# Gate tables in one fp32r product per token, the low part added at the eviction, five steps a body

## The chip, the cores and the metric

The kernel runs on one core of one Trainium2 chip. The metric is the device time of one execution in microseconds (us). Three executions of the kernel before took 3921.6, 3922.3 and 3922.45 us, so the median is 3922.3 us.

## The reference, cut to what matters

The model has two layers. Each is an attention block and a layer of single-row experts ("PEER"), both followed by a layer norm. The change is in the expert layer:

```python
def peer_ffn(x, wq, sub_keys, u, v):
    ...                                    # eidx: 128 chosen experts a token (8 heads x 16)
    g = jax.nn.softmax(top_s, -1)          # their gates
    def blk(inp):
        xt, et, gt = inp
        h = jnp.einsum('td,tkd->tk', xt, u[et]).astype(jnp.float32)
        a = gt * jax.nn.gelu(h, approximate=False)
        return jnp.einsum('tk,tkd->td', a.astype(v.dtype), v[et])
```

There are 128 x 128 = 16384 experts, and an expert's number is a pair of keys (i1, i2), each from 0 to 127. The sequence has 256 tokens, handled as two blocks of 128 (b = 0 and 1).

## The kernel before, in words

**No gathers.** The kernel computes every expert for every token and multiplies by a gate that is zero for the experts that a token did not choose. That needs a table of gates for each block of 128 tokens: `gates`, 128 partitions (first key) x 128 second keys x 128 tokens, with the token innermost in memory. It lies in the 16384 columns of `arena`, and one block's table is moved to DRAM before the other block's is built.

**How a table is built.** For one token, TensorE multiplies two one-hot matrices over its 128 selections: `oh1[k, i] = (first key of k is i)` and `oh2[k, i] = gate of k where the second key of k is i`. The product is that token's 128 x 128 gates. `TG = 4` tokens make one step, and `STEPS = 32` steps make a block's table. In a step GpSimd writes `oh1` (`first_keys`, four instructions on L1056), VectorE writes `oh2` (`second_keys`, four on L1514), TensorE makes four plain fp32 products of 128 columns into one PSUM bank (`gate_step`, L650), and ScalarE copies that bank into `gates` (`place_gates`, L956), where consecutive elements of one token are 512 bytes apart.

**What it runs beside.** The tables are built inside the first expert product, x times u. TensorE's fp32r format keeps fewer bits than fp32, so weights and activations are split into a high and a low part. For each half tile of u (1024 columns), ScalarE writes the high part (`split_hi`, L738), VectorE the low part (`split_lo`, L1100), and TensorE does `hidden(i, j)`: 8 products of 512 columns (L458) and 8 of 256 (L460). There are 4 buffers each for high and low, so the split of half j + 4 waits until TensorE has used half j. After each odd half ScalarE takes one part of the sum out (`take_cross`, L939), VectorE adds the other (`add_cross`, L1401), and ScalarE applies the GELU (L944).

**The order around the change.** All engines run lists written by hand, in bodies of eight halves, j = 0 to 7. The 32 bodies of a layer come in four quarters of eight. In the first and third VectorE also finds the top keys (`route_body`). The second and fourth are the build quarters, one for each block, so the program has four of them. The first body of a build quarter prepares the selections (`sel_t`, ready after j = 4) and does gate steps 0 and 1 after halves 6 and 7. Then five bodies do six steps each, at the places `STEP_OF = {0: 0, 1: 1, 3: 2, 4: 3, 6: 4, 7: 5}` (after half j, the step of that number in the body), and the last two do none. VectorE's `second_keys` for a step stands two halves ahead (`STEP_AHEAD`), and `oh1` and `oh2` have two buffers each: a step's one-hots may be written as soon as the step two before it is done.

The quantities are linked by semaphores: `oh1_done` and `oh2_done` (one-hots written), `gate_mm` (products done), `gate_evac` (bank free again). An engine that waits in its list holds everything behind the waiting instruction.

Of the kernel before, what the change touches and what calls it, by code (L numbers as in the profile page):

```python
# [15 lines left out]
P = 128  # L16
# [110 lines left out]
def build(nc, x_in, w_in, w_out, wq, keys, u_t, v_t, ln, sinks, lamp, subg, layer_consts,  # L127
# [13 lines left out]
    with ExitStack() as ctx:  # L141
# [9 lines left out]
        arena = sb("arena", [P, 16384])  # L151
        scr = sb("scr", [P, 4096])
# [85 lines left out]
        assert 2 + BUILD * PER_BODY == STEPS and BUILD < quarter - 1  # L238
        PIECES = 16
        ROWS = NKEY // PIECES  # L240
        oh1 = [scr[:, i * 512:(i + 1) * 512].rearrange("p (t n) -> p t n", n=NKEY) for i in range(2)]
        oh2 = [scr[:, 1024 + i * 512:1024 + (i + 1) * 512].rearrange("p (t n) -> p t n", n=NKEY)
               for i in range(2)]
# [5 lines left out]
        bank = [ctx.enter_context(nc.psum_tensor(f"bank{i}", [P, W], F32)) for i in range(8)]  # L249
# [33 lines left out]
        with nc.Block() as block:  # L283
            for layer in range(DEPTH):
# [18 lines left out]
                oh1_done, oh2_done, gate_mm, gate_evac = sem("oh1_done"), sem("oh2_done"), sem("gate_mm"), sem("gate_evac")  # L303
                gates_out, cols_done = sem("gates_out"), sem("cols_done")
# [120 lines left out]
                def _(pe):  # L425
# [230 lines left out]
                    for b in range(NB):  # L656
# [15 lines left out]
                        with pe.Fori(1, 1 + BUILD) as i:  # L672
                            for j in range(BODY):
                                hidden(i + (2 * b + 1) * quarter, j)
                                if j in STEP_OF:
                                    gate_step(i * PER_BODY + (b * STEPS + 2 - PER_BODY + STEP_OF[j]), STEP_OF[j] % 2)
                        with pe.Fori(1 + BUILD, quarter) as i:
                            for j in range(BODY):
                                hidden(i + (2 * b + 1) * quarter, j)
# [46 lines left out]
                def _(act):  # L726
# [246 lines left out]
                    for b in range(NB):  # L973
# [17 lines left out]
                        with act.Fori(1, 1 + BUILD) as i:  # L991
                            for j in range(BODY):
                                half_body(i + (2 * b + 1) * quarter, j)
                                if j in STEP_OF:
                                    at = 2 - PER_BODY + STEP_OF[j]
                                    place_gates(i * PER_BODY + (b * STEPS + at), i * (PER_BODY * TG) + at * TG, STEP_OF[j] % 2, b)
                        with act.Fori(1 + BUILD, quarter - (b == 1)) as i:
                            for j in range(BODY):
                                half_body(i + (2 * b + 1) * quarter, j)
# [29 lines left out]
                def _(pool):  # L1029
# [20 lines left out]
                    def first_keys(s, p, first=False):  # L1050
                        if not first:
                            pool.wait_ge(gate_mm, s - 1)
# [31 lines left out]
                def _(dve):  # L1084
# [457 lines left out]
                    STEP_AHEAD = {1: -2, 2: -1, 4: 0, 5: 1, 6: 2, 7: 3}  # L1542

                    def build_body(i, b, steps=STEP_AHEAD):

                        for j in range(BODY):
                            build_split(i, b, j)
                            if j in steps:
                                second_keys(i * PER_BODY + (b * STEPS + STEP_AHEAD[j]), STEP_AHEAD[j] % 2)

                    def first_build_body(b):

                        gate_weights(b)
                        for j in range(BODY):
# [5 lines left out]
                            if j >= 4:  # L1560
                                second_keys(b * STEPS + j - 4, j % 2, first=(b == 0 and j < 6))
# [12 lines left out]
                    for b in range(NB):  # L1574
# [3 lines left out]
                        with dve.Fori(1, BUILD) as i:  # L1578
                            build_body(i, b)
                        build_body(BUILD, b, steps=(1, 2, 4, 5))  # L1580
                        with dve.Fori(1 + BUILD, quarter - (b == 1)) as i:
                            build_body(i, b, steps=())
# [161 lines left out]
```

## Time and profile before

| | value |
|---|---|
| median of three runs | 3922.3 us |
| the profiled execution's own time | 3923.11 us |
| its span in the trace | 3921.3 us |
| TensorE (matmul) busy | 3872.0 us, 99% |
| VectorE busy | 2631.4 us, 67% |
| ScalarE busy | 2010.4 us, 51% |
| GpSimd busy | 509.5 us, 13% |
| granted TensorE clock, mean | 0.996 of 2.4 GHz |

The busy share of TensorE is that of overlapping records: a matmul's record begins when it starts and ends when its last result is out, and the next begins meanwhile. How long one takes in a row of many is therefore read from the distance between starts, and the same holds for the small overlap of VectorE's and ScalarE's records. The build quarters of the first layer lie at 679 to 823 us and at 1066 to 1210 us of the span, those of the second at 2630 to 2773 us and 3017 to 3160 us.

### The profile page before, as it was taken

To read this page: it belongs to the slowest core of one execution; us is meant where nothing else is said; L and a number is where in the kernel's file an instruction comes from. 1 tells how busy PE (TensorE), PEld (TensorE's weight loads), DVE (VectorE), ACT (ScalarE), POOL (GpSimd) and SP (SyncE) were. 2 spreads that over 40 slices of the span, in tenths; PEclk is the share of its full clock that TensorE was granted. 3 is DMA by queue.
4 is the path that set the end of the run, shared out by engine and by line. 5 is a ranking of instruction groups with operands and counts; after the bars stand their busy time and mean duration, and the time that the engine had idled before them with its cause. 6 is when DMAs were issued, how large, how long until landed. Compare 5 with 4: busy or idle time off the path is not lost.

```text
span 3921.3 us, 63614 instructions
## 1 busy us (share of the span) xinstructions
PE 3872.0 (99%) x20308; PEld 3291.4 (84%) x20308; DVE 2631.4 (67%) x4996; ACT 2010.4 (51%) x2936; POOL 509.5 (13%) x716
## 2 busy tenths in 40 slices
PE   8999999999999999999999999999999999999998
PEld 7778888988888888888787788889888988888886
DVE  7765688658865555555687566886688655555556
ACT  5674445654565444444456644456545654444443
POOL 1000001720172000000011000027102710000000
PEclk9999999999999999999999999999999999999999
DMA  6435466469645666666644454664685466666664
GB/s 226 160 140 202 174 210 211 169 203 282 216 169 205 231 229 230 229 229 229 224 172 151 148 207 175 207 206 173 213 275 205 170 216 228 229 229 229 229 230 170
DMA packets 244173, 806.64 MB, mean 206 GB/s; under 512 B 24928, under 2 KB 157536, under 8 KB 159328
## 3 DMA queue, kind: packets, MB, share of 16 engines
q1 hardware_dynamic: 207200, 771.65, 56.6%
q10 hardware_dynamic: 36864, 33.57, 2.5%
q8 instruction: 65, 1.06, 0.1%
q14 instruction: 44, 0.36, 0.0%
HBM read 752.69 MB, written 52.43 MB: 205 GB/s over the span
## 4 chain that ended last, share of the span: by engine, by line
PE 96%; DVE 2%; ACT 1%; POOL 1%; issue 0%; DMA 0%; ACTq 0%; SPq 0%; DVEq 0%; POOLq 0%
PE bank L458 27%; PE bank L460 14%; PE bank L688 12%; PE bank L690 12%; PE bank L689 12%; PE bank L472 5%; PE bank L474 5%; PE bank L473 5%; PE bank L650 3%; PE bank L500 1%; PE bank L513 1%; PE bank L529 0%; PE bank L627 0%; PE bank L485 0%; POOL scr L1056 0%; ACT hi L738 0%
## 5 line engine op out<-in xcount | busy, mean ns | idle before, releaser
L1100 DVE TENSOR_TENSOR lo<-raw,hi 128x1024 fp32r<-128x1024 f32 x1312 | 1613.5, 1230 | 1010.6 <-ACT hi L738 982.1
L738 ACT ACTIVATE hi<-raw 128x1024 fp32r<-128x1024 f32 x1312 | 1389.0, 1059 | 1464.8 <-PE bank L690 756.9
L458 PE MATMUL bank<-xhl,hi 128*128 128x512 f32 x4608 | 1199.6, 395 | 1.8 <-ACT scr L930 1.4
L458 PEld LDWEIGHTS bank<-xhl,hi 128*128 128x128 f32 x4608 | 813.7, 189 | 134.5 <-ACT scr L930 1.8
L688 PE MATMUL bank<-hi,xhl 128*128 128x512 f32 x2048 | 797.1, 389 | 3.0 <-DVE gelu_out L1401 2.7
L690 PE MATMUL bank<-hi,xhl 128*128 128x512 f32 x2048 | 796.7, 389 | 0.0
L689 PE MATMUL bank<-lo,xhl 128*128 128x512 f32 x2048 | 796.7, 389 | 0.0
L460 PEld LDWEIGHTS bank<-xhl,lo 128*128 128x128 f32 x4608 | 655.0, 190 | 64.0
L460 PE MATMUL bank<-xhl,lo 128*128 128x256 f32 x4608 | 671.6, 282 | 0.0
L688 PEld LDWEIGHTS bank<-hi,xhl 128*128 128x128 f32 x2048 | 384.4, 188 | 83.9 <-DVE gelu_out L1401 3.1
L690 PEld LDWEIGHTS bank<-hi,xhl 128*128 128x128 f32 x2048 | 384.4, 188 | 79.8
L689 PEld LDWEIGHTS bank<-lo,xhl 128*128 128x128 f32 x2048 | 384.4, 188 | 79.7
L1056 POOL TENSOR_SCALAR scr<-iota_k,small 128x128 f32<-128x128 f32 x512 | 410.7, 819 | 12.3
L472 PE MATMUL bank<-hi,xhl 128*128 128x512 f32 (+1 forms) x896 | 360.2, 402 | 3.8 <-DVE xhl L1118 3.7
L474 PE MATMUL bank<-hi,xhl 128*128 128x512 f32 (+1 forms) x896 | 349.8, 390 | 0.0
L473 PE MATMUL bank<-lo,xhl 128*128 128x512 f32 (+1 forms) x896 | 348.2, 389 | 0.0
L939 ACT ACTIVATE gelu_out<-bank 128x256 f32<-128x256 f32 x256 | 98.4, 384 | 304.7 <-PE bank L460 264.9
L472 PEld LDWEIGHTS bank<-hi,xhl 128*128 128x128 f32 x896 | 168.9, 188 | 39.0 <-issue 4.7
L474 PEld LDWEIGHTS bank<-hi,xhl 128*128 128x128 f32 x896 | 168.7, 188 | 35.8
L473 PEld LDWEIGHTS bank<-lo,xhl 128*128 128x128 f32 x896 | 169.3, 189 | 30.9
L1401 DVE TENSOR_TENSOR gelu_out<-bank,gelu_out 128x256 f32<-128x256 f32 x256 | 108.4, 423 | 119.2 <-ACT gelu_out L939 103.6
L956 ACT ACTIVATE arena<-bank 128x512 f32 (+1 forms) x128 | 142.0, 1109 | 47.4 <-ACT gelu_out L944 45.6
(153 smaller groups left out, 2208.4 us busy)
## 6 DMA issues: line engine op xcount, KB each, us to landing
raw<-u_t SPq DMA_DIRECT2D x256, 1024.0 KB, 5.0
raw<-v_t SPq DMA_DIRECT2D x256, 1024.0 KB, 4.8
raw<-w_in SPq DMA_DIRECT2D x80, 1024.0 KB, 4.8
raw<-w_out SPq DMA_DIRECT2D x32, 1024.0 KB, 4.8
raw<-wq SPq DMA_DIRECT2D x32, 1024.0 KB, 4.8
gelu_scratch<-gelu_out ACTq DMA_DIRECT2D x256, 128.0 KB, 3.7
scr<-gelu_scratch SPq DMA_DIRECT2D x256, 128.0 KB, 4.6
gates_scratch<-arena SPq DMA_DIRECT2D x32, 512.0 KB, 9.7
```

The costliest lines, as they stand in the source:

```text
L458: pe.matmul(acc[:], w, xhl[:, c, :, :].rearrange("p a t -> p (a t)"), start=(c == 0), stop=False)
L460: last = pe.matmul(acc[:, L:2 * L], w, xh[:, c, :], start=False, stop=(c == DC - 1))
L472: pe.matmul(banks[b][:, 0:width], st_h, mh, start=(c == first_c), stop=False)
L473: pe.matmul(banks[b][:, 0:width], st_h, ml, start=False, stop=False)
L474: last = pe.matmul(banks[b][:, 0:width], st_l, mh, start=False, stop=(c == last_c))
L688: pe.matmul(y, a_h, vh, start=start, stop=False)
L689: pe.matmul(y, a_h, vl, start=False, stop=False)
L690: last = pe.matmul(y, a_l, vh, start=False, stop=stop)
L738: act.activation(hi[j % NSPLIT][:], half, ACT.Copy).then_inc(hi_done, 1)
L956: act.activation(gates.rearrange("p i t -> p t i")[:, bass.ds(col, TG), :], bank[4 + p][:].rearrange("p (t i) -> p t i", t=TG), ACT.Copy). ...
L1056: last = pool.tensor_scalar(oh1[p][:, t, :], iota_k[:], key_cols[p][:, t:t + 1], None, ALU.is_equal)
L1100: dve.tensor_tensor(lo[j % NSPLIT][:], half, hi[j % NSPLIT][:].bitcast(F32), ALU.subtract).then_inc(lo_done, 1)
```

## The change

The gate is split into a high part (rounded to fp32r) and a low remainder, once for a block (`split_shares`). `oh2` of a token now is 256 columns, the high share beside the low one, written by one instruction on VectorE. TensorE makes one fp32r product of 256 columns a token. ScalarE places the high table as before, and VectorE then adds the low table from PSUM into `gates` (`add_low`), after which the banks are free. A step fills two banks, and steps alternate between two pairs. The 256-column `oh2` has room for four tokens in all, one step, and is given back by halves: two tokens of a step may be written when the same two of the step before are multiplied. `oh1` still has two buffers. Six bodies do five steps each.

```diff
-        STEP_OF = {0: 0, 1: 1, 3: 2, 4: 3, 6: 4, 7: 5}
+        STEP_OF = {0: 0, 1: 1, 3: 2, 5: 3, 6: 4}
+        PAIRS_AT = {0: 1, 1: 2, 3: 3, 5: 4, 6: 5}
+        LOW_AT = {1: 0, 2: 1, 4: 2, 6: 3, 7: 4}
...
                     def gate_step(s, p, first=False):
                         pe.wait_ge(oh1_done, s + 1)
-                        pe.wait_ge(oh2_done, s + 1)
                         if not first:
                             pe.wait_ge(gate_evac, s - 1)
-                        for t in range(TG):
-                            last = pe.matmul(bank[4 + p][:, t * P:(t + 1) * P], oh1[p][:, t, :], oh2[p][:, t, :],
-                                             start=True, stop=True)
-                        last.then_inc(gate_mm, 1)
+                        for half in range(2):
+                            pe.wait_ge(oh2_done, s * 2 + (half + 1))
+                            for t in range(2):
+                                last = pe.matmul(bank[4 + 2 * p + half][:, t * 2 * P:(t + 1) * 2 * P], oh1[p][:, 2 * half + t, :],
+                                                 oh2[:, 2 * half + t, :, :].rearrange("p r n -> p (r n)"), start=True, stop=True)
+                            last.then_inc(gate_mm, 1)
...
                     def place_gates(s, col, p, b):
-                        act.wait_ge(gate_mm, s + 1)
+                        act.wait_ge(gate_mm, s * 2 + 2)
...
-                                       bank[4 + p][:].rearrange("p (t i) -> p t i", t=TG), ACT.Copy).then_inc(gate_evac, 1)
+                                       pair_gates[p][:, 0], ACT.Copy).then_inc(gate_high, 1)
...
-                    def second_keys(s, p, first=False):
-                        if not first:
-                            dve.wait_ge(gate_mm, s - 1)
-                        for t in range(TG):
-                            col = s * TG + t
-                            last = dve.tensor_scalar(oh2[p][:, t, :], iota_k[:], sel_t[:, 1, bass.ds(col, 1)],
-                                                     sel_t[:, 2, bass.ds(col, 1)], ALU.is_equal, ALU.mult)
-                        last.then_inc(oh2_done, 1)
-
+                    def split_shares(b):
+                        gate = sel_t[:, 2, b * P:(b + 1) * P]
+                        own(mark(dve.tensor_copy(cand[:, 0:P].bitcast(F32R), gate)))
+                        own(mark(dve.tensor_tensor(cand[:, P:2 * P], gate, cand[:, 0:P], ALU.subtract)))
+
+                    def second_keys(b, s, first=False):
+                        for half in range(2):
+                            if not first:
+                                dve.wait_ge(gate_mm, s * 2 + (2 * b * STEPS + half - 1))
+                            for t in range(2 * half, 2 * half + 2):
+                                col = s * TG + t
+                                last = dve.scalar_tensor_tensor(
+                                    out=oh2[:, t], in0=iota_k[:].unsqueeze(1).to_broadcast([P, 2, NKEY]),
+                                    scalar=sel_t[:, 1, bass.ds(col + b * P, 1)],
+                                    in1=shares[:, :, bass.ds(col, 1)].to_broadcast([P, 2, NKEY]), op0=ALU.is_equal, op1=ALU.mult)
+                            last.then_inc(oh2_done, 1)
+
+                    def add_low(b, s, p):
+                        dve.wait_ge(gate_high, s + (b * STEPS + 1))
+                        cols = gates.rearrange("p i t -> p t i")[:, bass.ds(s * TG, TG), :]
+                        dve.tensor_tensor(cols, cols, pair_gates[p][:, 1], ALU.add).then_inc(gate_evac, 1)
...
                         for j in range(BODY):
                             build_split(i, b, j)
-                            if j in steps:
-                                second_keys(i * PER_BODY + (b * STEPS + STEP_AHEAD[j]), STEP_AHEAD[j] % 2)
+                            if j in LOW_AT:
+                                add_low(b, step + LOW_AT[j], (PER_BODY * odd + LOW_AT[j]) % 2)
+                            if j in PAIRS_AT and not (last and PAIRS_AT[j] == PER_BODY):
+                                second_keys(b, step + PAIRS_AT[j])
```

In the first body of a build quarter, VectorE splits the shares and writes step 0's one-hots at j = 4, step 1's at j = 6, and after j = 7 it does `add_low` of steps 0 and 1 and only then the one-hots of step 2.

On TensorE, the start of the loop's body before. L458 and L460 are one hidden half, L650 is one gate step.

```order
L458 MATMUL bank<-xhl,hi 128x512 x8
L460 MATMUL bank<-xhl,lo 128x256 x8
L645 ISA
L648 REGISTER_ALU
L650 MATMUL bank<-scr 128x128 x4
L634 REGISTER_ALU
L458 MATMUL bank<-xhl,hi 128x512 x8
L460 MATMUL bank<-xhl,lo 128x256 x8
L645 REGISTER_ALU
L648 REGISTER_ALU
L650 MATMUL bank<-scr 128x128 x4
```

The same place now; L466 and L468 are the hidden half, L659 the gate products, `one_hots` holds `oh1` and `oh2`, and `upper` is the four upper PSUM banks.

```order
L466 MATMUL bank<-xhl,hi 128x512 x8
L468 MATMUL bank<-xhl,lo 128x256 x8
L653 ISA
L655 REGISTER_ALU
L657 ISA
L659 MATMUL upper<-one_hots 128x256 x2
L657 REGISTER_ALU
L659 MATMUL upper<-one_hots 128x256 x2
L642 REGISTER_ALU
L466 MATMUL bank<-xhl,hi 128x512 x8
L468 MATMUL bank<-xhl,lo 128x256 x8
```

One run of four products became two runs of two, with a wait for VectorE ahead of each.

On VectorE, the end of a build quarter's first body before: L1514 is `second_keys` (of steps 0 to 3).

```order
L1100 TENSOR_TENSOR lo<-raw,hi 128x1024 x2
L1514 TENSOR_SCALAR scr<-iota_k,sel_t 128x128 x4
L1401 TENSOR_TENSOR gelu_out<-bank,gelu_out 128x256
L1100 TENSOR_TENSOR lo<-raw,hi 128x1024
L1514 TENSOR_SCALAR scr<-iota_k,sel_t 128x128 x4
L1100 TENSOR_TENSOR lo<-raw,hi 128x1024
L1514 TENSOR_SCALAR scr<-iota_k,sel_t 128x128 x4
L1401 TENSOR_TENSOR gelu_out<-bank,gelu_out 128x256
L1100 TENSOR_TENSOR lo<-raw,hi 128x1024
L1514 TENSOR_SCALAR scr<-iota_k,sel_t 128x128 x4
```

The same place now: L1111 is the low split, L1412 `add_cross`, L1522 and L1523 split the shares, L1531 is `second_keys` (of steps 0 to 2), L1540 is `add_low`.

```order
L1111 TENSOR_TENSOR lo<-raw,hi 128x1024 x2
L1522 CAST cand<-sel_t 128x128
L1523 TENSOR_TENSOR cand<-sel_t,cand 128x128
L1531 SCALAR_TENSOR_TENSOR one_hots<-iota_k,sel_t,cand 128x256 x4
L1412 TENSOR_TENSOR gelu_out<-bank,gelu_out 128x256
L1111 TENSOR_TENSOR lo<-raw,hi 128x1024 x2
L1531 SCALAR_TENSOR_TENSOR one_hots<-iota_k,sel_t,cand 128x256 x4
L1412 TENSOR_TENSOR gelu_out<-bank,gelu_out 128x256
L1111 TENSOR_TENSOR lo<-raw,hi 128x1024
L1540 TENSOR_TENSOR arena<-arena,upper 128x4x128 x2
L1531 SCALAR_TENSOR_TENSOR one_hots<-iota_k,sel_t,cand 128x256 x4
```

The one-hots of step 1 moved from j = 5 to j = 6, those of step 2 from j = 6 to behind j = 7, and two `add_low` stand ahead of them.

## Rows read from the trace of the kernel before

**Rows 1.** The page, busy time of each engine, its share of the span, instructions.

```profile
PE 3872.0 (99%) x20308; PEld 3291.4 (84%) x20308; DVE 2631.4 (67%) x4996; ACT 2010.4 (51%) x2936; POOL 509.5 (13%) x716
```

**Rows 2.** The page, the chain that ended last, by engine.

```profile
PE 96%; DVE 2%; ACT 1%; POOL 1%; issue 0%; DMA 0%; ACTq 0%; SPq 0%; DVEq 0%; POOLq 0%
```

**Rows 3.** Waits from 676 to 880 us: who for whom, us, times, longest.

```profile
DVE lo L1100 <- ACT hi L738: 50.1, 61, 2.2
...
PE bank L650 <- POOL scr L1056: 0.4, 1, 0.4
```

**Rows 4.** The chain from 760 to 800 us: start, us, what.

```profile
762.01 0.95 PE bank L460 x8
762.96 0.89 PE bank L650 x8
...
774.94 1.85 PE bank L458 x8
776.78 0.95 PE bank L460 x8
```

**Rows 5.** Timeline in a build body, after an even half: start, us, engine.

```profile
770.19 1.05 PE L650 MATMUL bank<-scr 128*128 128x128 f32 x8
...
770.39 1.06 ACT L738 ACTIVATE hi<-raw 128x1024 fp32r<-128x1024 f32 x1 [1.35 <-PE bank L460]
...
771.48 1.22 DVE L1100 TENSOR_TENSOR lo<-raw,hi 128x1024 fp32r<-128x1024 f32 x1 [1.11 <-ACT hi L738]
```

**Rows 6.** The same after an odd half, and VectorE behind a split.

```profile
780.57 0.39 ACT L939 ACTIVATE gelu_out<-bank 128x256 f32<-128x256 f32 x1 [1.43 <-PE bank L460]
780.85 1.05 ACT L738 ACTIVATE hi<-raw 128x1024 fp32r<-128x1024 f32 x1
...
785.35 1.23 DVE L1100 TENSOR_TENSOR lo<-raw,hi 128x1024 fp32r<-128x1024 f32 x1 [2.20 <-ACT hi L738]
786.49 1.23 DVE L1514 TENSOR_SCALAR scr<-iota_k,sel_t 128x128 f32<-128x128 f32 x4
```

**Rows 7.** Timeline of VectorE: a two-input instruction with a scalar, and adds in a row.

```profile
2044.78 0.47 DVE L1248 SCALAR_TENSOR_TENSOR sel_t<-scr,small,sel_t 128x256 f32<-128x256 f32 x1
2045.17 1.21 DVE L1100 TENSOR_TENSOR lo<-raw,hi 128x1024 fp32r<-128x1024 f32 x1
...
431.29 1.41 DVE L1396 TENSOR_TENSOR arena<-bank,arena 128x256 f32<-128x256 f32 x4
```

**Rows 8.** The same instruction beside GpSimd, which started at 87.19 us.

```profile
87.03 2.43 DVE L1248 SCALAR_TENSOR_TENSOR sel_t<-scr,small,sel_t 128x128 f32<-128x128 f32 x4
...
87.19 1.33 POOL L1041 TENSOR_TENSOR scr<-scr 128x512 f32<-128x512 f32 x1 [18.95 <-DVE scr L1141]
```

**Rows 9.** The one-hots before, by line: min/median/max ns.

```profile
L1514 DVE TENSOR_SCALAR scr<-iota_k,sel_t x512: 332/341/418, 675.6 to 3157.1; 128x128 f32<-128x128 f32 x171
...
L1056 POOL TENSOR_SCALAR scr<-iota_k,small x512: 597/602/1692, 676.0 to 3154.0; 128x128 f32<-128x128 f32 x171
```

**Rows 10.** Groups by line and shape: busy us, mean ns, idle before.

```profile
L1514 DVE TENSOR_SCALAR scr<-iota_k,sel_t 128x128 f32<-128x128 f32 x512 | 151.4, 357 | 0.0
L956 ACT ACTIVATE arena<-bank 128x512 f32 x120 | 133.1, 1109 | 45.6 <-ACT gelu_out L944 45.6
...
L1139 DVE TENSOR_TENSOR scr<-bank,arena 128x512 f32<-128x512 f32 x28 | 19.2, 686 | 11.1 <-PE bank L474 8.6 <-issue 2.5
...
L930 ACT ACTIVATE scr<-bank 128x512 f32<-128x512 f32 x16 | 9.1, 609 | 2.4 <-PE bank L627 2.4
```

**Rows 11.** Timeline at the first build quarter's opening, and one VectorE-to-TensorE hand-over.

```profile
679.46 1.16 PE L650 MATMUL bank<-scr 128*128 128x128 f32 x8 [0.36 <-POOL scr L1056]
...
679.64 3.43 POOL L1056 TENSOR_SCALAR scr<-iota_k,small 128x128 f32<-128x128 f32 x4
...
13.14 0.69 DVE L1118 TENSOR_TENSOR xhl<-scr,xhl 128x512 fp32r<-128x512 f32 x1 [0.27 <-ACT xhl L764]
13.89 0.29 PEld L472 LDWEIGHTS bank<-hi,xhl 128*128 128x128 f32 x1 [4.08 <-DVE xhl L1118]
```

More of the change, by code:

```diff
@@ L247, in build @@
         prod = [scr[:, 3584 + i * L:3584 + (i + 1) * L] for i in range(2)]
-        bank = [ctx.enter_context(nc.psum_tensor(f"bank{i}", [P, W], F32)) for i in range(8)]
+        upper = ctx.enter_context(nc.psum_tensor("upper", [P, 4 * W], F32))
+        bank = [ctx.enter_context(nc.psum_tensor(f"bank{i}", [P, W], F32)) for i in range(4)]
+        bank += [upper[:, i * W:(i + 1) * W] for i in range(4)]
+        pair_gates = [upper[:, p * 2 * W:(p + 1) * 2 * W].rearrange("p (t r i) -> p r t i", r=2, i=NKEY) for p in range(2)]
         eye_in, iota_in = (ctx.enter_context(nc.semaphore(n)) for n in ("eye_in", "iota_in"))
@@ L671, in _ @@
                                 gate_step(b * STEPS + j - 6, j % 2, first=(b == 0))
[L672 to L679, printed above, removed]
+                        with pe.Fori(0, BUILD // 2) as i:
+                            for odd in range(2):
+                                for j in range(BODY):
+                                    hidden(i * 2 + ((2 * b + 1) * quarter + 1 + odd), j)
+                                    if j in STEP_OF:
+                                        at = 2 + PER_BODY * odd + STEP_OF[j]
+                                        gate_step(i * (2 * PER_BODY) + (b * STEPS + at), at % 2)
+                        for j in range(BODY):
+                            hidden((2 * b + 2) * quarter - 1, j)
                     def products(b, j, slot, start=False, stop=False, qs=(0, 1)):
@@ L990, in _ @@
                                 place_gates(b * STEPS + j - 6, (j - 6) * TG, j % 2, b)
-                        with act.Fori(1, 1 + BUILD) as i:
-                            for j in range(BODY):
[L993 to L999, printed above, removed]
+                        with act.Fori(0, BUILD // 2) as i:
+                            for odd in range(2):
+                                for j in range(BODY):
+                                    half_body(i * 2 + ((2 * b + 1) * quarter + 1 + odd), j)
+                                    if j in STEP_OF:
+                                        at = 2 + PER_BODY * odd + STEP_OF[j]
+                                        place_gates(i * (2 * PER_BODY) + (b * STEPS + at), i * (2 * PER_BODY * TG) + at * TG, at % 2, b)
+                        if b == 0:
+                            for j in range(BODY):
+                                half_body(2 * quarter - 1, j)
                     def a_high(i, m):
@@ L1540, in build_split, with build_body @@
                             split_lo(AT_U, i + (2 * b + 1) * quarter + ahead // BODY, ahead % BODY)
[L1542 to L1544 removed]
+                    def build_body(i, b, step, odd, last=False):
                         for j in range(BODY):
                             build_split(i, b, j)
[L1548 to L1549 removed]
+                            if j in LOW_AT:
+                                add_low(b, step + LOW_AT[j], (PER_BODY * odd + LOW_AT[j]) % 2)
+                            if j in PAIRS_AT and not (last and PAIRS_AT[j] == PER_BODY):
+                                second_keys(b, step + PAIRS_AT[j])
                     def first_build_body(b):
@@ L1559, in first_build_body @@
                                 dve.wait_ge(sel_stored, b + 1)
-                            if j >= 4:
-                                second_keys(b * STEPS + j - 4, j % 2, first=(b == 0 and j < 6))
+                                split_shares(b)
+                                second_keys(b, 0, first=(b == 0))
+                            if j == 6:
+                                second_keys(b, 1)
+                        add_low(b, 0, 0)
+                        add_low(b, 1, 1)
+                        second_keys(b, 2)
                     def last_build_body():
@@ L1577, in _ @@
                         first_build_body(b)
[L1578 to L1582, printed above, removed]
+                        with dve.Fori(0, BUILD // 2 - 1) as i:
+                            for odd in range(2):
+                                build_body(i * 2 + (1 + odd), b, i * (2 * PER_BODY) + (2 + PER_BODY * odd), odd)
+                        build_body(BUILD - 1, b, STEPS - 2 * PER_BODY, 0)
+                        build_body(BUILD, b, STEPS - PER_BODY, 1, last=True)
+                        if b == 0:
+                            for j in range(BODY):
+                                build_split(quarter - 1, b, j)
                     last_build_body()
```

13 lines of the change are left out of this document (8 added, 5 removed).

## The prediction

> **What bounds the kernel now.** I read the page first. TensorE is busy 99% of the span, VectorE 67%, GpSimd 13% [rows 1], and the chain that ended last is 96% TensorE [rows 2]. The list of waits inside the first build quarter says the same more sharply: VectorE waits 61 times for ScalarE's high part, while TensorE waits once, 0.4 us, for the first one-hots [rows 3]. So a microsecond taken off TensorE there is a microsecond of the end, as long as its one-hots and low parts still come in time. Whether they do is the whole question, because the change takes work off TensorE and puts more on VectorE, with less lead.
>
> **TensorE's part.** In the chain, a hidden half takes 1.85 + 0.95 = 2.80 us, and a gate step takes 0.89 us from its first start to that of the next product [rows 4]. A new step is four fp32r products of 256 columns, each with its own weights. That is the same kind of instruction as the eight of L460, which take 0.95 us, 0.119 each [rows 4], so a step becomes 4 x 0.119 = 0.48 us. It saves 0.41 us. A build quarter has 32 steps, so 13.1 us, and the four quarters 52.5 us. If nothing came late, this would be the result.
>
> **VectorE's new prices.** The trace has no such one-hot instruction. One two-input instruction with a scalar from memory on 256 elements was followed by the next after 0.39 us (2044.78 to 2045.17) [rows 7]. Plain adds of 256 elements run at 0.33 us each (four in 1.41 us, the last record of 0.42 included), which is the lower bound. Beside a running GpSimd instruction, four of the two-input kind on only 128 elements took 2.43 us, 0.60 each [rows 8], which is the upper bound. The old one-hots, also written beside GpSimd, average 357 ns where the shortest is 332 [rows 9, 10]. I add that 0.03 to 0.39 and take **S = 0.42 us**, near the row of the same kind and size.
>
> `add_low` (**A**) reads PSUM and reads and writes the table at 512-byte steps. Contiguous, such an add of 512 elements takes 686 ns [rows 10], 0.61 from start to start. ScalarE's eviction into the same places takes 1109 ns against 609 for a contiguous one of this size [rows 10], so the steps cost it 0.50 us. The upper bound pays this for the read and for the write, 0.61 + 1.00 = 1.6 us. I take them as overlapping, 0.61 + 0.50 = **1.11 us**, close to ScalarE's own row. The Trainium skill ("Vector Engine (DVE) Microarchitecture Reference", measured stream behaviour on trn2) says that a stream that hops at every element slows its port, that read and write penalties only partly add, and gives 1.98 ns a column where all three hop. By that, A would be about 1.09 us and the total 0.2 us less. The trace agrees only through ScalarE's row.
>
> Per body VectorE then does 8 splits at 1.14 (785.35 to 786.49) [rows 6], 4 `add_cross` at 0.33, and 5 x (4S + A) = 13.95: together 24.4 us. TensorE's body is 8 x 2.80 + 5 x 0.48 = 24.8 us. VectorE fits on average, but barely, so what counts is when each piece is due.
>
> **What is late: one-hots due one half later.** There is room for one step of `oh2`, so step n + 1 is written after step n is multiplied. Most steps are two halves apart, but steps 0 and 1 of a body (after j = 0 and 1) and steps 3 and 4 (after j = 5 and 6) are one half apart. I follow the first pair, counting from the end of hidden half 0.
>
> - ScalarE starts the high split at 0.20 (770.19 to 770.39), VectorE's split starts 1.09 after that, at 1.29 [rows 5], and ends at 2.43. The one-hots stand behind it in VectorE's list. The first pair is written at 2.43 + 2S + 0.08 = 3.35, the second at 4.19.
> - TensorE does gate step 0 (0.48) and hidden half 1 (2.80), and wants step 1 at 3.28. From the end of a VectorE record to the weight load that waited for it took 0.06 (13.83 to 13.89) [rows 11]. A gate step that had waited had a record of 1.16 [rows 11] instead of 1.05 [rows 5], so I add 0.09 for a restart. The first two products end at 3.74, and the second two start at 4.34 and end at 4.58. In time it would have been 3.76, so TensorE loses **0.82 us** (4S - 0.86).
> - After j = 5 ScalarE first does `take_cross`, 0.28 us more (780.57 to 780.85) [rows 6]. The same walk gives **1.10 us** (4S - 0.58).
>
> The other three steps of a body are due after two halves, some 6 us after the step before, and come in time. GpSimd's four one-hots take 3.43 us [rows 11], and with two buffers they are due after three halves. The high split of half j + 4 has three halves of lead and stays in time. ScalarE does one eviction a body less. So a body loses 1.92 us of the 2.05 that its five steps save.
>
> **The opening of a quarter.** The first gate step waits for GpSimd as before (its start at 679.46 includes that) [rows 11]. The second now is due one half later, at about 682.8, and GpSimd's second one-hots end at 679.64 + 3.43 = 683.07 [rows 11]: 0.38 with the restart. Then the third: hidden half 7 ends at 679.46 + 0.57 + 2.80 = 682.83, and by the walk for an odd half VectorE is through its split at 682.83 + 1.57 + 1.14 = 685.54, and two `add_low` (2A) and four one-hots (4S) stand ahead. The last two products end at 689.91, where 686.97 would be in time: **2.94 us** (2A + 4S - 0.96). VectorE is then so far on that step 1 of the next body is not late. The share split costs VectorE 0.6 us where it is ahead of need.
>
> **The sum.** One quarter: -13.12 + 6 x 1.10 + 5 x 0.82 + 0.38 + 2.94 = **+0.90 us**, or in general 48S + 2A - 21.5. The four quarters make +3.6 us. Against the profiled execution's own 3923.11 us this is 3926.7. The median of the runs is 0.8 us lower, so I forecast **3926 us**. It is a difference of two sums of about 50 us: S moves it by 1.9 us for each 0.01, A by 0.8 for each 0.1.
>
> Outside the build quarters nothing changes: the table of block 0 is complete about one body later, still ahead of where SyncE's list stores it.
>
> **The rivals.**
>
> *The one-hots cost no more than plain adds.* With S = 0.33 and A = 0.61, a quarter gives 15.84 + 1.22 - 21.48 = -4.4, together -18 us: 3905. For it: the broadcast operands are nothing dear in the row of 0.39, and perhaps the scalar is cheaper here. Against it: that same row is already 0.06 above an add.
>
> *TensorE stays the bound and keeps its gain.* -52 us: 3870. For it: VectorE fits on average. Against it: one-hots cannot be written before the step ahead of them, and in the list they stand behind a split that starts at 1.29.
>
> *VectorE and GpSimd get in each other's way.* The old instruction read one tensor, the new one reads two, while GpSimd is writing its own one-hots most of the time. If each pays as in the row of 0.60 us [rows 8], a quarter costs 28.8 + 2.22 - 21.48 = +9.5. VectorE's body is then 10.4 + 12 + 5.6 = 28.0 us, over TensorE's 24.8 plus waits, which adds about 1.6: some +45 us, 3967. It decides from S = 0.44 on, where the result passes +0.2%. For it: GpSimd's instruction of 602 ns reaches 1692 [rows 9], so they do collide. Against it: VectorE's two-input split beside GpSimd still is 1.14 [rows 6], so there GpSimd paid. The Trainium skill ("SBUF — State Buffer", who interferes with whom) states that a VectorE instruction with two SBUF inputs contends with a GpSimd instruction that reads SBUF. By it, this rival is what the new one-hots invite; the trace shows it in rows 8 and not in rows 6.
>
> *`add_low` saturates VectorE.* With A = 1.6 a body of VectorE is 10.4 + 8.4 + 8.0 = 26.8 us, as long as TensorE's with its waits. The lateness is carried on, about 3 us a quarter beyond the formula's +1.9: +20 us, 3942.
>
> *The product is no cheaper.* If a 256-column product cost what the fp32 one did, only the losses would remain, 3978. Against it: L460.
>
> **How the numbers follow.** This measurement can hardly tell 0.2%, 7.8 us, from no change. My own case (S from 0.37 to 0.44) has 0.40 and gives 3916 to 3934. Cheap one-hots have 0.21, the kept gain 0.06, contention 0.14, saturation 0.15, the dear product 0.04. Faster by over 0.2% is cheap one-hots, the kept gain and a little of my own case: 0.29. Slower is contention, saturation and the dear product, less the mild ends of the first two: 0.30. Within 0.2%: 0.41. The range for 8 in 10 leaves out the kept gain, the dear product and the worst of the contention: 3900 to 3950.
>
> **What would show it.** In the profile after: L659 at 0.119 us a product; TensorE waiting on VectorE's L1531 twice a body, 0.8 and 1.1 us, and about 3 us once a quarter; L1531 at 0.42 from start to start and L1540 at 1.11; the splits never waited for. I am wrong if the waits on L1531 are absent or above 3 us a body, if TensorE waits for GpSimd in the loop, or if it waits for L1111's low part.

## The result: 0.4% slower, and the profile after

The changed kernel takes 3938.5 us (median of 6 runs, 3937.3 to 3939.0), the kernel before 3922.5 us (6 runs). The ratio is 1.0040, with a 95% interval of 1.0030 to 1.0051. That is 12.5 us above the forecast of 3926, inside its range of 3900 to 3950, outside the 3916 to 3934 of my own case, and on the side of "slower by over 0.2%", which had a chance of 0.30. One slow execution of e1 below (7754 us) and one of e3 (13799 us) are left out of every ratio.

The page of the kernel after, busy time of each engine, its share of the span, instructions. Beside [rows 1]:

```profile
PE 3848.6 (98%) x19796; PEld 3247.7 (83%) x19796; DVE 2860.7 (73%) x5132; ACT 2011.2 (51%) x2936; POOL 566.0 (14%) x716
```

TensorE's records cover 23 us less and VectorE's 229 us more. The chain that ended last [rows 2] no longer is TensorE's alone:

```profile
PE 88%; DVE 6%; ACT 2%; issue 2%; POOL 1%; DVEq 0%; DMA 0%; ACTq 0%; SPq 0%; POOLq 0%
```

In the list of waits (us in total, times, longest us) the first line is new; the second was 1.4 us for 4 times:

```profile
PE upper L659 <- DVE one_hots L1531: 33.8, 76, 2.2
...
PE upper L659 <- POOL one_hots L1067: 4.3, 8, 0.8
```

This list counts only the time in which no matmul record is open, and each record outlasts the start of the next product by 0.16 us and more. So the waits are better read from the distance of starts. The timeline of TensorE at the first quarter's opening (start, us, engine; [rows 11] is the same place before):

```profile
685.53 2.00 PE L466 MATMUL bank<-xhl,hi 128*128 128x512 f32 x8
687.37 1.11 PE L468 MATMUL bank<-xhl,lo 128*128 128x256 f32 x8
690.57 0.61 PE L659 MATMUL upper<-one_hots 128*128 128x256 f32 x2 [2.09 <-DVE one_hots L1531]
691.40 0.79 PE L659 MATMUL upper<-one_hots 128*128 128x256 f32 x2 [0.22 <-DVE one_hots L1531]
691.99 3.05 PE L466 MATMUL bank<-xhl,hi 128*128 128x512 f32 x8
694.88 1.11 PE L468 MATMUL bank<-xhl,lo 128*128 128x256 f32 x8
695.83 0.64 PE L659 MATMUL upper<-one_hots 128*128 128x256 f32 x4
696.31 2.00 PE L466 MATMUL bank<-xhl,hi 128*128 128x512 f32 x8
```

Three things are in it. The last two rows give the new price of a step, 696.31 - 695.83 = 0.48 us, as forecast. Step 2 was due at 687.37 + 0.95 = 688.32 and could have ended at 688.80. It started at 690.57 and ended at 691.99. And then eight products of 512 columns took 2.89 us (691.99 to 694.88) where they otherwise take 1.84. The stretches by engine say why (the number behind the counts is the granted clock):

```profile
692.00:694.00 2.00, 2.00 (x6) 1.61 (x6) 2.00 (x5) 1.07 (x1) 1.54 (x3) 0.50 0.04 13
694.00:700.00 6.00, 6.00 (x36) 5.29 (x36) 3.24 (x5) 3.04 (x4) 4.68 (x8) 0.98 0.07 8
```

TensorE was granted 1.2 GHz instead of 2.4 for 3.4 us behind the long wait, and the second of the late pairs already took 0.59 us (691.40 to 691.99) where it otherwise takes 0.35. So some 0.24 of the step's 3.19 us of delay is the clock's, and the rest the wait's. The half rate came in three of the four build quarters. VectorE at the same place (it was idle for 0.53 us before the split at 686.05, and not again until these one-hots were written):

```profile
686.05 1.23 DVE L1111 TENSOR_TENSOR lo<-raw,hi 128x1024 fp32r<-128x1024 f32 x1 [0.53 <-ACT hi L748]
687.20 2.55 DVE L1540 TENSOR_TENSOR arena<-arena,upper 128x512 f32<-128x512 f32 x2
689.65 1.69 DVE L1531 SCALAR_TENSOR_TENSOR one_hots<-iota_k,sel_t,cand 128x256 fp32r<-128x256 f32 x4
```

In the loop, both late steps of a body, TensorE and VectorE:

```profile
721.12 1.11 PE L468 MATMUL bank<-xhl,lo 128*128 128x256 f32 x8
722.30 0.50 PE L659 MATMUL upper<-one_hots 128*128 128x256 f32 x2
723.12 0.51 PE L659 MATMUL upper<-one_hots 128*128 128x256 f32 x2 [0.32 <-DVE one_hots L1531]
723.47 1.99 PE L466 MATMUL bank<-xhl,hi 128*128 128x512 f32 x8
...
737.43 1.11 PE L468 MATMUL bank<-xhl,lo 128*128 128x256 f32 x8
738.94 0.50 PE L659 MATMUL upper<-one_hots 128*128 128x256 f32 x2 [0.40 <-DVE one_hots L1531]
```
```profile
720.09 1.25 DVE L1111 TENSOR_TENSOR lo<-raw,hi 128x1024 fp32r<-128x1024 f32 x1
721.26 1.81 DVE L1531 SCALAR_TENSOR_TENSOR one_hots<-iota_k,sel_t,cand 128x256 fp32r<-128x256 f32 x4
```

Step 1 of the body was due at 721.12 + 0.95 = 722.07 and could end at 722.55. It ended at 723.47: 0.92 us late. The same reading of step 4 gives 1.25 us, and 1.49 in a quarter's first loop body.

The quarter's very first step (step 0 of the opening) is late too, and by more than before. GpSimd, and the step that waited for it:

```profile
677.25 3.84 POOL L1067 TENSOR_SCALAR one_hots<-iota_k,small 128x128 fp32r<-128x128 f32 x4
681.14 0.75 PE L659 MATMUL upper<-one_hots 128*128 128x256 f32 x4 [0.78 <-POOL one_hots L1067]
```

Its four one-hots took 3.84 us where they took 3.43 before (and 3.58 for step 1), and the step cost 1.03 us beyond its price, where it cost 0.54 before.

The groups by line and shape (busy us, mean ns, idle before), beside [rows 10]:

```profile
L1531 DVE SCALAR_TENSOR_TENSOR one_hots<-iota_k,sel_t,cand 128x256 fp32r<-128x256 f32 x512 | 225.3, 498 | 0.1
L966 ACT ACTIVATE arena<-upper 128x512 f32 x120 | 133.1, 1109 | 45.0 <-PE upper L659 27.8 <-ACT gelu_out L954 15.8
L1540 DVE TENSOR_TENSOR arena<-arena,upper 128x512 f32 x80 | 109.6, 1370 | 0.0
```

One one-hot instruction is 225.3 / 512 = 0.44 us, where I took 0.42. An `add_low` record is 1.37 us, 1.28 from start to start, where I took 1.11.

**The sum, from these rows.** I added up, over each quarter, what the hidden halves (2.79 us) and steps (0.48 us) took beyond their price, from start to start. Before, a half with a step took 3.69 us (771.00 to 774.69 on L458), so a step cost 0.90 and the saving is 0.42.

| us a quarter | forecast | measured, four quarters |
|---|---|---|
| saved by the products | 13.1 | 13.4 (32 x 0.42) |
| opening, step 0, beyond the 0.54 of before | 0 | 0.49 |
| opening, step 1 | 0.38 | 0.54 |
| opening, step 2 | 2.94 | 2.92 to 3.02 |
| step 4 of a body, six times | 1.10 | 1.49, then 1.24, the last 1.10 |
| step 1 of a body, five times | 0.82 | 0.91 |
| all waits | 14.0 | 16.0 |
| half-rate clock | 0 | 1.3, 1.55, 1.56, 0 |

Four quarters: 64.1 + 4.4 - 53.8 = +14.7 us. Read directly, from the half ahead of step 0 to the 56th half behind it, a quarter took 185.85 us before and 189.66, 189.93, 189.95 and 188.47 after, 14.6 us more in all. The spans differ by 15.2 us (3936.5 and 3921.3).

### The profile page after: what moved, and what is told of

The parts are those of the page before. It is cut to its first block, busy times and chain, and to the rows that moved or that the text cites. A ratio compares the mean times of both kernels' runs of the same rounds, so it can differ in the third digit from the quotient of the medians.

```text
span 3936.5 us, 62878 instructions
## 1 busy us (share of the span) xinstructions
PE 3848.6 (98%) x19796; PEld 3247.7 (83%) x19796; DVE 2860.7 (73%) x5132; ACT 2011.2 (51%) x2936; POOL 566.0 (14%) x716
## 4 chain that ended last, share of the span: by engine, by line
PE 88%; DVE 6%; ACT 2%; issue 2%; POOL 1%; DVEq 0%; DMA 0%; ACTq 0%; SPq 0%; POOLq 0%
PE bank L466 21%; PE bank L468 11%; PE bank L698 6%; PE bank L700 6%; PE bank L699 6%; PE upper L698 6%; PE upper L700 6%; PE upper L699 6%; PE bank L480 5%; PE bank L482 5%; PE bank L481 5%; DVE one_hots L1531 2%; ACT hi L748 2%; PE upper L466 2%; DVE lo L1111 1%
## 5 line engine op out<-in xcount | busy, mean ns | idle before, releaser
L1111 DVE TENSOR_TENSOR lo<-raw,hi 128x1024 fp32r<-128x1024 f32 x1312 | 1614.9, 1231 | 870.3 <-ACT hi L748 839.4
L466 PE MATMUL bank<-xhl,hi 128*128 128x512 f32 x4352 | 1111.0, 394 | 1.8 <-ACT scr L940 1.4
L466 PEld LDWEIGHTS bank<-xhl,hi 128*128 128x128 f32 x4352 | 777.8, 189 | 135.1 <-ACT scr L940 1.8
L468 PEld LDWEIGHTS bank<-xhl,lo 128*128 128x128 f32 x4352 | 608.4, 191 | 51.8
L468 PE MATMUL bank<-xhl,lo 128*128 128x256 f32 x4352 | 622.3, 282 | 0.0
L1067 POOL TENSOR_SCALAR one_hots<-iota_k,small 128x128 fp32r<-128x128 f32 x512 | 440.9, 878 | 12.3
L698 PE MATMUL bank<-hi,xhl 128*128 128x512 f32 x1024 | 398.7, 389 | 3.0 <-DVE gelu_out L1412 2.6
L700 PE MATMUL bank<-hi,xhl 128*128 128x512 f32 x1024 | 398.4, 389 | 0.0
L699 PE MATMUL bank<-lo,xhl 128*128 128x512 f32 x1024 | 398.3, 389 | 0.0
L698 PE MATMUL upper<-hi,xhl 128*128 128x512 f32 x1024 | 398.3, 389 | 0.0
L699 PE MATMUL upper<-lo,xhl 128*128 128x512 f32 x1024 | 398.3, 389 | 0.0
L700 PE MATMUL upper<-hi,xhl 128*128 128x512 f32 x1024 | 398.3, 389 | 0.0
L698 PEld LDWEIGHTS bank<-hi,xhl 128*128 128x128 f32 x1024 | 192.2, 188 | 43.9 <-DVE gelu_out L1412 3.1
L1531 DVE SCALAR_TENSOR_TENSOR one_hots<-iota_k,sel_t,cand 128x256 fp32r<-128x256 f32 x512 | 225.3, 498 | 0.1
L700 PEld LDWEIGHTS bank<-hi,xhl 128*128 128x128 f32 x1024 | 192.2, 188 | 40.1
L699 PEld LDWEIGHTS upper<-lo,xhl 128*128 128x128 f32 x1024 | 192.3, 188 | 39.9
L698 PEld LDWEIGHTS upper<-hi,xhl 128*128 128x128 f32 x1024 | 192.2, 188 | 40.0
```

The source lines that it names most:

```text
L466: pe.matmul(acc[:], w, xhl[:, c, :, :].rearrange("p a t -> p (a t)"), start=(c == 0), stop=False)
L468: last = pe.matmul(acc[:, L:2 * L], w, xh[:, c, :], start=False, stop=(c == DC - 1))
L698: pe.matmul(y, a_h, vh, start=start, stop=False)
L699: pe.matmul(y, a_h, vl, start=False, stop=False)
L700: last = pe.matmul(y, a_l, vh, start=False, stop=stop)
L1067: last = pool.tensor_scalar(oh1[p][:, t, :], iota_k[:], key_cols[p][:, t:t + 1], None, ALU.is_equal)
```

## The experiments

All ran beside the kernel before, whose medians there were 3922.8 to 3923.2 us. "The waits" of a quarter below are counted as "all waits" in the table; the changed kernel has 16.0 us. My theory was list order: TensorE waits because the one-hots stand behind a split or an add in VectorE's list while they are due one half later. Its rival was that VectorE is full.

**Early one-hots everywhere (e1_early_all).** `build_split` gets the one-hots as an argument and puts them ahead of its split, for steps 1 and 4 of each body and for steps 1 and 2 of the opening:

```diff
 def build_split(i, b, j, last=False, keys=None):
     if j % 2:
         add_cross(...)
+    if keys:
+        keys()
     split_lo(...)
...
-    build_split(i, b, j)
+    early = j in (0, 5)
+    build_split(i, b, j, keys=(lambda: second_keys(b, step + PAIRS_AT[j])) if early else None)
...
-    if j in PAIRS_AT and not (last and PAIRS_AT[j] == PER_BODY):
+    if j in PAIRS_AT and not early and not (last and PAIRS_AT[j] == PER_BODY):
         second_keys(b, step + PAIRS_AT[j])
...
-    build_split(0, b, j)
+    if j == 7:
+        add_low(b, 0, 0)
+    build_split(0, b, j, keys={6: lambda: second_keys(b, 1), 7: lambda: second_keys(b, 2)}.get(j))
...
-    if j == 6:
-        second_keys(b, 1)
-    add_low(b, 0, 0)
     add_low(b, 1, 1)
-    second_keys(b, 2)
```

> One-hots of steps 1 and 4 of a body ahead of VectorE's split, and in the first body those of steps 1 and 2 ahead of the splits, with the second low add last. List order (my theory: TensorE waits 16.0 us a quarter because the one-hots stand behind a split or an add): the waits on L1531 go, about 61 us, and with them the half-rate clock stretches, 4 us: 3873 us. Saturation (VectorE's body of 8 x 1.14 + 4 x 0.33 + 5 x 3.02 = 25.5 us is longer than TensorE's 24.8): TensorE waits for the low splits in place of the one-hots, 0.7 us a body in 24 bodies: 3890 us.

Measured: 3892.5 us, ratio to before 0.9921 (0.9901 to 0.9941). So 46 us came from the order of one list alone, and the kernel is faster than both. But 20 us of what list order alone would give (3873) is missing, and both theories have a share. The waits are 5.3 to 5.7 us a quarter. Some 1.5 us of that are steps 1 and 2 of the opening, which I had expected to vanish, 6 us in all. In the loop it is now the second pair of a step that is late, 0.3 to 0.45 us twice a body, 3.3 to 3.8 us a quarter and 14 us in all. And VectorE, over most of the first quarter, is (PE, PEld, DVE, ACT, POOL busy):

```profile
700.00:830.00 130.00, 128.95 (x759) 113.49 (x758) 129.62 (x189) 81.97 (x108) 92.10 (x131) 1.00 0.52 182
```

129.62 of 130 us. It is full. With S = 0.44 and A = 1.28 its body is 9.1 + 1.3 + 5 x 3.04 = 25.6 us against TensorE's 24.8. The loop bodies of e1 take 25.4 to 25.6 us (739.40, 764.95 and 790.31 are the starts of three), so the 14 us are VectorE's. In the changed kernel's own order that shortage was hidden by TensorE's waits, which made the body 27 us long.

**Only the loop (e2_early_loop), only the opening (e3_early_opening).** The two halves of that edit.

> Only the loop's one-hots (steps 1 and 4 of a body) ahead of the split; the opening of a quarter stays. List order: 12.3 us less a quarter, 3889 us; the wait of 3.2 us at the opening and the half-rate stretches behind it stay. Saturation: 3906 us or more.

> Only the first body of a quarter is reordered; the loop's waits of 0.9 and 1.25 us stay. List order: the 3.2 us wait goes, 0.9 us comes at step 1 of the next body, which was spared before, so 2.5 us less a quarter; if the clock falls because of that wait, the 1.1 to 1.6 us behind it in three quarters go too: 3924 us, and no half rate in the build quarters. If the clock falls for another reason (the wait for GpSimd just before, or the sum of the waits): 3928 us, with the half rate still there.

Measured: 3902.0 us (0.9947; 0.9931 to 0.9964) and 3927.5 us (1.0012; 1.0002 to 1.0022). The first lies between its two cases: in e2 the waits are 6.9 to 8.1 us a quarter, the step-2 wait is still 2.9 us in three quarters (2.1 in the fourth), and the half rate follows it in two. The second has the number of the case with the half rate, but not its cause: there is no half rate in any quarter of e3. Its waits are 14.5 us a quarter, because the step after the opening was 1.5 us late and not 0.9, and step 1 of the opening 0.74 and not 0.54, which together are 3 us. The 1.03 us at step 0, behind GpSimd, are still there, so it is not that wait that brings the half rate:

```profile
690.55 1.11 PE L468 MATMUL bank<-xhl,lo 128*128 128x256 f32 x8
692.89 0.74 PE L659 MATMUL upper<-one_hots 128*128 128x256 f32 x4 [1.23 <-DVE one_hots L1531]
693.47 2.00 PE L466 MATMUL bank<-xhl,hi 128*128 128x512 f32 x8
695.31 1.11 PE L468 MATMUL bank<-xhl,lo 128*128 128x256 f32 x8
```

After this wait of 1.5 us the next eight products still take 1.84 (693.47 to 695.31).

**A low add of 8 elements (e4_low_8).**

```diff
-dve.tensor_tensor(cols, cols, pair_gates[p][:, 1], ALU.add)
+dve.tensor_tensor(cols[:, 0, 0:8], cols[:, 0, 0:8], pair_gates[p][:, 1, 0, 0:8], ALU.add)
```

> The low add covers 8 elements instead of 512, so the low table is left out but for these; every instruction and wait stays in its place. List order: the opening's wait shrinks by two adds, 2.4 us, the first body's by 0.2, the waits of 0.9 and 1.25 us a body stay; with the clock back, 3924 us. Saturation: the loop's waits shrink too, towards 0.5 us a body: 3890 us.

Measured: 3925.4 us (1.0005; 0.9995 to 1.0015), as list order said. The opening's step 2 is 0.6 to 0.8 us late in three quarters (1.0 in the fourth) instead of 3.0, the half rate is gone, the 1.49 us of the first late step fall to 1.24, and the other waits of the loop stay at 0.91 and 1.24 us. So in the changed order the add costs the loop nothing: what is late there stands behind the split, not behind the add.

**GpSimd writes 8 columns of its one-hots (e5_pool_8).** From step 2 on:

```diff
-last = pool.tensor_scalar(oh1[p][:, t, :], iota_k[:], key_cols[p][:, t:t + 1], None, ALU.is_equal)
+last = pool.tensor_scalar(oh1[p][:, t, 0:8], iota_k[:, 0:8], key_cols[p][:, t:t + 1], None, ALU.is_equal)
```

> The changed kernel in its own order, but GpSimd writes only 8 of the 128 columns of each one-hot from step 2 on, so it hardly touches memory beside VectorE (the tables are then partly stale). If GpSimd makes VectorE's one-hots dear (contention), they fall from 0.43 to the 0.39 from start to start, and TensorE's loop waits from 0.92 and 1.25 to 0.75 and 1.1 us: 3930 us. If 0.43 is what the instruction costs (my theory), nothing moves: 3938 us.

Measured: 3930.1 us (1.0023; 1.0013 to 1.0032). This is the number of the contention theory, and mine, that 0.43 is what the instruction costs by itself, fell. The number alone would say too much, though. VectorE's one-hots by line, and a late four of them in the loop, which took 1.81 us before:

```profile
L1531 DVE SCALAR_TENSOR_TENSOR one_hots<-iota_k,sel_t,cand 128x256 fp32r<-128x256 f32 x512 | 215.5, 481 | 0.1
```
```profile
747.45 1.70 DVE L1531 SCALAR_TENSOR_TENSOR one_hots<-iota_k,sel_t,cand 128x256 fp32r<-128x256 f32 x4
```

Four now take 1.70 us, 0.41 from start to start instead of 0.44. The waits fall from 16.0 to 14.8 us in three quarters (13.9 in the fourth), which is 5 to 6 us. The half rate appears in one quarter instead of three, the other 3 us, but that is not shown to be GpSimd's doing: the opening's step 2 is 2.92 us late in the second and third quarter, as in the changed kernel, where the half rate followed. The ten executions also fall into two groups, 3928.6 to 3930.1 and 3933.5 to 3935.1 us, and the profile is of the lower one.

**A contiguous low add (e6_contig).** On top of e1_early_all:

```diff
-dve.tensor_tensor(cols, cols, pair_gates[p][:, 1], ALU.add)
+dve.tensor_tensor(pair_gates[p][:, 1], iota_k[:].unsqueeze(1).to_broadcast([P, TG, NKEY]), pair_gates[p][:, 1], ALU.add)
```

> Early one-hots as in e1_early_all, and the low add keeps its 512 elements but reads a contiguous SBUF operand and writes back to PSUM, so no operand is strided and the low part does not reach the table. Strides (my theory): the add falls from 1.28 to 0.65 us, VectorE's body from 25.5 to 22.4 us, under TensorE's 24.8; the waits of about 0.4 us twice a body that stay in e1_early_all go: 3877 us. If these waits are the hand-over between engines and not a full VectorE: 3892 us as e1_early_all.

Measured: 3879.9 us (0.9890; 0.9873 to 0.9906). The add is 685 ns, and the loop's waits are gone. What is left, 2.2 us a quarter, lies in the opening. The 12.6 us between this kernel and e1_early_all are what a full VectorE had cost, and the strides had filled it; the rest of the missing 20 us is the opening, which stays.

**High and low added up in PSUM (e7_psum_sum).** On top of e1_early_all, with `add_low` left out and `gate_evac` given by the eviction:

```diff
-    last = pe.matmul(bank[4 + 2 * p + half][:, t * 2 * P:(t + 1) * 2 * P], oh1[p][:, 2 * half + t, :],
-                     oh2[:, 2 * half + t, :, :].rearrange("p r n -> p (r n)"), start=True, stop=True)
+    for r in range(2):
+        last = pe.matmul(bank[4 + 2 * p + half][:, t * 2 * P:t * 2 * P + P], oh1[p][:, 2 * half + t, :],
+                         oh2[:, 2 * half + t, r, :], start=(r == 0), stop=(r == 1))
```

> Early one-hots as in e1_early_all, but high and low product of a token are two products of 128 columns added up in the same PSUM columns, so the low add is gone from VectorE and the whole table is kept. If a 128-column fp32r product costs TensorE half of a 256-column one (0.06 us), a step stays 0.48 us and VectorE has room: 3877 us. If it costs as much as one of 256 columns (0.12 us), a step takes 0.95 us: 3932 us. If it costs as a 128-column fp32 product (0.205 us), a step takes 1.6 us: 4020 us.

Measured: 3929.4 us (1.0016; 1.0006 to 1.0026), near the middle case. TensorE in the loop:

```profile
743.40 1.01 PE L660 MATMUL upper<-one_hots 128*128 128x128 f32 x8
744.25 2.07 PE L466 MATMUL bank<-xhl,hi 128*128 128x512 f32 x8
```

Eight products of 128 columns take 0.85 us, 0.106 each, almost what one of 256 columns takes (0.119). From half to half, a step adds 0.90 us, just as the old fp32 one did. The gain of the change is therefore that high and low lie side by side in one wide product, and not the format alone; and the low add is its price.

**Four tokens innermost (e8_t_inner_early, e9_t_inner).** The token is innermost in the table, and a step has four of them. Walking the table with the token innermost gives runs of four adjacent elements, and the jumps move to the PSUM side. The first is on top of e1_early_all, the second on the changed kernel in its own order; both keep the whole table:

```diff
-cols = gates.rearrange("p i t -> p t i")[:, bass.ds(s * TG, TG), :]
-dve.tensor_tensor(cols, cols, pair_gates[p][:, 1], ALU.add).then_inc(gate_evac, 1)
+cols = gates[:, :, bass.ds(s * TG, TG)]
+dve.tensor_tensor(cols, cols, pair_gates[p][:, 1].rearrange("p t i -> p i t"), ALU.add).then_inc(gate_evac, 1)
...
-act.activation(gates.rearrange("p i t -> p t i")[:, bass.ds(col, TG), :], pair_gates[p][:, 0], ACT.Copy)
+act.activation(gates[:, :, bass.ds(col, TG)], pair_gates[p][:, 0].rearrange("p t i -> p i t"), ACT.Copy)
```

> Early one-hots as in e1_early_all, whole tables kept; the eviction and the low add walk the table with the four tokens innermost, so in SBUF runs of 4 adjacent elements take the place of single ones 512 bytes apart, and PSUM is read at steps of 1024 bytes instead. If single hops in SBUF make the add dear (my theory) and a hop in PSUM is cheap: the add falls from 1.28 to about 0.65 us, as in e6_contig, 3880 us. If the PSUM hop costs the same: the add stays above 1.1 us, 3892 us.

> The same walk in the changed kernel's own order. By the list order the add is only in TensorE's way in the first body: 1.2 us less at step 2 and 0.2 at the next late step, a quarter; 3933 us with the half-rate stretches, 3929 us if the shorter wait spares them. The loop's waits of 0.92 and 1.25 us stay. If a full VectorE caused those, they shrink: below 3915 us.

Measured: **3877.6 us** (0.9886; 0.9869 to 0.9902) and 3927.3 us (1.0010; 1.0001 to 1.0020). The groups of e8:

```profile
L966 ACT ACTIVATE arena<-upper 128x512 f32 x120 | 71.2, 593 | 37.9 <-ACT gelu_out L954 34.3 <-PE upper L659 2.5 <-issue 1.1
L1540 DVE TENSOR_TENSOR arena<-arena,upper 128x512 f32 x80 | 54.1, 676 | 0.0
```

The add falls from 1370 to 676 ns and ScalarE's eviction from 1109 to 593, the price of contiguous ones. VectorE has room again and TensorE is busy throughout (e8, same stretch as above):

```profile
700.00:830.00 130.00, 130.00 (x778) 115.90 (x777) 119.30 (x196) 70.57 (x111) 106.22 (x130) 1.00 0.56 192
```

What is left is 1.9 to 2.2 us a quarter in the opening: 8.4 - 53.8 = -45.4 us. The medians differ by 45.5 us (3877.6 and 3923.2). e9 shows how little the cheaper add is worth while the order is wrong: the loop's waits stay at 0.91 and 1.24 us, step 2 of the opening is 1.7 to 1.8 us late in three quarters, and the half rate is gone.

## Why the prediction was right, and what it missed

**The gain and the mechanism were right.** A step costs 0.48 us (forecast 0.48), and 53.8 us are saved where 52.5 were forecast. The loss is where the walk through the lists put it: the third gate step of a quarter, and the two steps of a body that are due one half later. Moving only those one-hots in VectorE's list (e1) gave back 46 us. Nothing else waited in the loop: not the splits, nor GpSimd's one-hots.

**The size was not.** The kernel became 16 us slower, where 3.6 were forecast, and my own case ended at 3934. The forecast was a difference of two sums of some 50 us, so small errors decided its size, and they happened to lie on one side. The range held because it left room for rivals that did not come as they were told.

- *The waits, 56 us forecast, 64.1 measured.* The step "I add that 0.03 to 0.39 and take S = 0.42": it measures 0.44, and in the late steps four take 1.81 us, which is 0.445 from start to start. The restart of 0.09 was short as well: the rows it came from differ by 1.16 - 1.05 = 0.11, and a late pair takes 0.35 us (723.12 to 723.47) instead of 0.24. The split ahead of them started a little late too. Together it is 0.09 us and 0.14 us a step.
- *"I take them as overlapping, 0.61 + 0.50 = 1.11 us"*: A measures 1.28. It cost little in this order (0.25 us at the first late step of a quarter, which e4 takes away), but it is what fills VectorE in e1. The contiguous and the short-run add (0.685 and 0.676 us) show that all of the extra is the strides.
- *"The first gate step waits for GpSimd as before"*: GpSimd's four one-hots take 3.84 and then 3.58 us in the opening, not 3.43. With the restart that is 0.65 us a quarter over steps 0 and 1.
- *The clock was not in the sum.* 4.4 us. The forecast had TensorE waiting 3 us at one place and priced it at 3 us.

With S = 0.44 and A = 1.28 the forecast's own formula gives +2.2 us a quarter, 8.8 in all. The opening's 2.6 us, the clock's 4.4 and the 1.3 us more that the products saved make it 14.5, and the build quarters measure 14.6.

**The rivals.** Contention was a rival at S = 0.60 and +45 us. It exists at a small part of that: GpSimd's one-hots lengthen VectorE's by about 0.02 us on average and 0.03 in the loop, which is some 5 us of the result (e5; that run still has GpSimd's short instructions in it). GpSimd pays more, 878 ns a one-hot against 819 before, and up to 1919. And the 0.60 itself was a misreading. The line of rows 8 is four records merged under the shape of the first; asked one by one, two have 128 columns and two have 256, and a single one was long:

```profile
87.03 0.34 DVE L1248 SCALAR_TENSOR_TENSOR sel_t<-scr,small,sel_t 128x128 f32<-128x128 f32 x1
87.29 1.51 DVE L1248 SCALAR_TENSOR_TENSOR sel_t<-scr,small,sel_t 128x256 f32<-128x256 f32 x1
88.73 0.34 DVE L1248 SCALAR_TENSOR_TENSOR sel_t<-scr,small,sel_t 128x128 f32<-128x128 f32 x1
88.99 0.47 DVE L1248 SCALAR_TENSOR_TENSOR sel_t<-scr,small,sel_t 128x256 f32<-128x256 f32 x1
```

So it was not 0.60 for each, but 1.04 us once, beside a GpSimd instruction of 1.33 us. Beside GpSimd's one-hots no instruction of L1531 took more than 0.60 us. The Trainium skill ("SBUF — State Buffer", who interferes with whom) says that a VectorE instruction with two SBUF inputs contends with a GpSimd one that reads SBUF. The trace agrees in kind, and the size is 0.03 us of 0.44.

Saturation was a rival at A = 1.6. At 1.28 it did not decide this kernel (e4: the loop's waits hardly move when the add is cut), but it cost e1 some 13 us. The kept gain of -52 us was called excluded by the list; with the list changed, e8 gets 45 of it. Cheap one-hots and the dear product did not come.

The Trainium skill's rule on strides ("Vector Engine (DVE) Microarchitecture Reference", measured stream behaviour on trn2) has a half that I had not used: a port keeps its full rate when elements come in runs of two or more adjacent words that start on an 8-byte boundary. The trace agrees: runs of four gave 676 ns against 1370.

## What to carry to other kernels

When work moves to an engine that has room on average, read its instruction list at each hand-over: what stands ahead of the awaited instruction, and how long before it is due. Moving a few calls in one list was worth 46 us here, more than the change itself lost. Then count the full engine again with the waits gone, since a wait elsewhere can hide that it is over its limit. A merged line of a timeline carries the shape of its first record alone, so look at the records before taking their mean as a price. And when a table is written in strides, look whether another walk gives short runs of neighbours before paying for the jumps.

## What the runs showed of the hardware that I had not expected

- **A single long wait can cost more than itself.** Where a step was 2.9 to 3.0 us late, the granted clock fell to 0.50 for 3.4 us in 3 of 4 quarters of the changed kernel, 2 of 3 in e2 and 1 of 3 in e5, and each time 1.3 to 1.6 us were lost. In the fourth quarters of e2 and e5 (2.1 and 2.0 us) and in the 24 quarters of e1, e3, e4, e6, e8 and e9, where no wait is above 1.8 us, it did not happen. Why it comes in some quarters and not in others stays open.
- **A 128-column fp32r product is hardly cheaper than a 256-column one:** 0.106 and 0.119 us (e7), and a step of eight of them adds the same 0.90 us as one of four 128-column fp32 products did before.
- **The same kind of instruction can be held up once or slowed a little.** A VectorE instruction with two SBUF inputs took 1.51 us instead of 0.47 beside one GpSimd instruction of 512 elements (87.29 us, kernel before), while beside the one-hots it was GpSimd that was held up, by up to 1.3 us (1919 ns against a shortest of 597), and VectorE by 0.03. Which of the two waits, and why, stays open.
- **Jumps in PSUM were free, jumps in SBUF were not.** An add or a copy of 512 elements reading PSUM at steps of 1024 bytes and walking SBUF in runs of four took 676 and 593 ns; with single elements 512 bytes apart in SBUF and PSUM contiguous, 1370 and 1109 ns (e8).
